# Norm of the latents ahead of the last gate tile's end, a new buffer layout, and head roots spread by rounded hi/lo products

## What is computed

```python
z = h @ w_in
qa, ka, va, cq, ckv, kpe, gate = jnp.split(z, ATT_SPLITS, axis=-1)
cq = _rmsnorm(cq, g_qa)                  # 512 latents
q_nope = jnp.einsum('bsc,chd->bshd', cq, w_uq)
q_pe = _rope(jnp.einsum('bsc,chr->bshr', cq, w_uqr), pos)
ckv = _rmsnorm(ckv, g_kva)
kpe = _rope(kpe[:, :, None, :], pos)[:, :, 0, :]
...
o_a = _diff_attention(qa, k_all, v_all, lam, q_chunk, k_chunk)
o_a = _rmsnorm(o_a, g_subln, SUBLN_EPS) * (1.0 - lam_init)   # per head
o_lat = _mla_attention(q_lat, q_pe, ckv_all, kpe_all, q_chunk, k_chunk)
o_b = jnp.einsum('bshc,chv->bshv', o_lat, w_uv)
o = jnp.concatenate([o_a, o_b], axis=-1) * jax.nn.silu(gate)
y = o @ w_out
```

## Time and profile before

| | us |
|---|---|
| median of 3 runs | 2079.89 |
| lowest and highest | 2076.95, 2081.9 |
| profiled execution, device time | 2074.99 |
| its span | 2073.2 |
| PE busy | 1850.0 (89%) |
| DVE busy | 1255.5 (61%) |
| ACT busy | 411.3 (20%) |
| POOL busy | 197.4 (10%) |

### The profile page before, as it was taken

The page is one execution under the profiler, slowest core; times in us unless marked ns, Lnnn a source line. Parts: engine busy times, 40 slices in busy tenths (PEclk is TensorE's granted clock), DMA queues, the critical chain, the costliest instruction groups (busy, mean ns, idle before and its releaser), DMA issues.

```text
span 2073.2 us, 32711 instructions
## 1 busy us (share of the span) xinstructions
PE 1850.0 (89%) x13182; PEld 1699.9 (82%) x13182; DVE 1255.5 (61%) x1598; ACT 411.3 (20%) x912; POOL 197.4 (10%) x117
## 2 busy tenths in 40 slices
PE   5548999999999978997987899968999999999995
PEld 0108999999999966776876778957999999999995
DVE  4899667667867653554355544376777544584444
ACT  1241000000010012332355443431000000131111
POOL 2770000000600000000000011210000000001110
PEclk8879999999999999998889898989999999999997
DMA  9555555545655422216134244214444333452222
GB/s 388 226 223 192 205 191 212 193 189 193 238 205 209 182 102 62 62 32 178 60 113 138 84 143 173 91 61 158 180 182 187 126 108 120 163 194 86 81 81 86
DMA packets 86104, 316.04 MB, mean 152 GB/s; under 512 B 12184, under 2 KB 20552, under 8 KB 60448
## 3 DMA queue, kind: packets, MB, share of 16 engines
q1 hardware_dynamic: 64208, 237.70, 31.6%
q10 hardware_dynamic: 21200, 76.48, 10.3%
q0 software_dynamic: 640, 1.10, 0.1%
HBM read 282.56 MB, written 32.69 MB: 152 GB/s over the span
## 4 chain that ended last, share of the span: by engine, by line
PE 66%; DVE 14%; DMA 7%; issue 5%; ACT 5%; POOL 2%; SPq 0%; DVEq 0%; ACTq 0%; POOLq 0%
PE banks L718 66%; DVE banks L1604 3%; DMA w_raw<-in_w_pin 3%; POOL ssq L676 2%; DMA w_adr<-in_w_ada_dve 2%; DMA w_more<-in_w_ada_pe 1%; ACT pxd L1387 1%; DMA d_raw<-pool_d_scratch 1%; DVE w_hi L1566 1%; DVE std L1839 1%; DVE h_lo L395 1%; DVE rstd L1546 1%; DVE x L2034 1%; ACT px L1305 0%; DVE pt_lo L1773 0%
## 5 line engine op out<-in xcount | busy, mean ns | idle before, releaser
L718 PE MATMUL banks<-h_hi,w_hi 128*128 128x272 f32 x3968 | 830.2, 295 | 61.0 <-DVE w_lo L1567 29.5
L718 PE MATMUL banks<-h_lo,w_hi 128*128 128x272 f32 x3712 | 776.4, 291 | 0.0
L718 PE MATMUL banks<-h_hi,w_lo 128*128 128x272 f32 x3456 | 716.1, 289 | 0.0
L718 PEld LDWEIGHTS banks<-h_hi,w_hi 128*128 128x128 f32 x3968 | 630.6, 193 | 72.5 <-issue 45.9
L718 PEld LDWEIGHTS banks<-h_lo,w_hi 128*128 128x128 f32 x3712 | 594.1, 192 | 0.0
L718 PEld LDWEIGHTS banks<-h_hi,w_lo 128*128 128x128 f32 x3456 | 545.5, 190 | 0.0
L1604 DVE CUSTOM_DVE_ANT_0 banks<-w_adr,cond_b 128x2048 f32<-128x2048 f32 x160 | 386.2, 2414 | 19.0 <-DMA w_adr<-in_w_ada_dve 15.8
L1566 DVE CAST w_hi<-w_raw 128x2048 fp32r<-128x2048 f32 x101 | 125.6, 1244 | 219.7 <-PE banks L718 168.2
L1567 DVE TENSOR_TENSOR w_lo<-w_raw,w_hi 128x2048 fp32r<-128x2048 f32 x101 | 249.2, 2467 | 3.5
L1251 ACT ACTIVATE stage<-banks 128x544 f32<-128x544 f32 x48 | 30.1, 627 | 514.4 <-PE banks L718 514.4
L1927 DVE TENSOR_TENSOR x<-x,stage 128x544 f32 (+1 forms) x32 | 23.9, 748 | 168.3 <-ACT stage L1469 168.3
(11 more groups left out here) (293 smaller groups left out, 1696.6 us busy)
## 6 DMA issues: line engine op xcount, KB each, us to landing
w_adr<-in_w_ada_dve ACTq DMA_DIRECT2D x46, 1024.0 KB, 5.0
w_adr<-in_w_ada_dve SPq DMA_DIRECT2D x34, 1024.0 KB, 4.9
w_raw<-in_w_z SPq DMA_DIRECT2D x32, 1024.0 KB, 6.2
w_raw<-in_w_pin SPq DMA_DIRECT2D x32, 1024.0 KB, 6.0
w_raw<-in_w_gate SPq DMA_DIRECT2D x16, 1024.0 KB, 6.9
w_raw<-in_w_out SPq DMA_DIRECT2D x32, 512.0 KB, 3.8
w_raw<-in_w_pout SPq DMA_DIRECT2D x16, 1024.0 KB, 4.8
w_more<-in_w_ada_pe SPq DMA_DIRECT2D x10, 1024.0 KB, 7.4
```

The costliest lines, as they stand in the source:

```text
L718: return pe.matmul(out, lhsT, rhs, start=start, stop=stop)
```

## The change

It has four parts. (1) The sums over partitions and the norm of cq and ckT are put ahead of the last gate tile's end: PE makes the sums between gate tiles 14 and 15, into banks 4 to 7, and no longer waits for the rotation of kpe before the MLA items; ACT's square roots stand between its evictions of these two tiles; DVE works out the norm before it waits for the last tile and its store. SP asks for the first MLA weights after the last adaLN product, and waits for tile and stores only ahead of the gates `sg`. (2) The layout of the MLA and differential scopes is new, so that the factors and the first MLA weights lie over nothing that is still read. The clearing of `qps` comes after the norm. (3) `widen` multiplies rounded operands: `sel_rnd` (rounded by ACT), `rs_hi` and `rs_lo`, four matmuls for a head in place of two in float32, in three bank pairs in place of two; all eight steps of latent half tile 15 come before the first of them. (4) On SP, `qds`, `kds` and `vcs` for the first pair are loaded later, `sel_row` earlier, and the last four rows of x only when all heads are scaled.

```diff
@@ sync @@
-            sp.wait_ge(mm_done, G_OUT)
             sp.wait_ge(adr_used, ADA_P0 + ADA_P1)
-            for s in range(2):
-                sp.wait_ge(stored[s], 16 * (ZT + GT) // 2)
...
                 if t == 0:
+                    sp.wait_ge(mm_done, G_OUT)
+                    for s in range(2):
+                        sp.wait_ge(stored[s], 16 * (ZT + GT) // 2)
                     load_sg(0)
...
             load_head(0)
             load_head(1)
-            for z0, dst in ((ZQ, qds), (ZK, kds), (ZV, vds)):
-                sp.dma_start(dst[:], z_out[z0:z0 + HEADS, :, NP:R].rearrange("h p r -> p h r")).then_inc(new_in, 16)
+            sp.dma_start(vds[:], z_out[ZV:ZV + HEADS, :, NP:R].rearrange("h p r -> p h r")).then_inc(vds_in, 16)
             load_cache(0)
-            load_vcache(0)
...
             sp.wait_ge(ms_fin, 1)
             sp.wait_ge(latent_out, 32)
+            for z0, dst in ((ZQ, qds), (ZK, kds)):
+                sp.dma_start(dst[:], z_out[z0:z0 + HEADS, :, NP:R].rearrange("h p r -> p h r")).then_inc(new_in, 16)
+            load_vcache(0)
...
             sp.wait_ge(df_pv, HEADS)
+            sp.dma_start(sel_row[:], selr).then_inc(df_r_in, 16)
...
             for s in range(2):
                 sp.wait_ge(x1_out[s], 16 * KT // 2)
+            sp.wait_ge(df_scaled, HEADS)
@@ tensor @@
-            big_loop(G_GATE, 0, GT // 2)
-            for s in range(2):
-                pe.wait_ge(acc_free[s], turn_of(G_OUT + (G_OUT + s) % 2))
+            big_loop(G_GATE, 0, GT // 2 - 1)
+            big_wait(G_GATE + GT - 2)
+            big_tile((G_GATE + GT - 2) % 2)
             pe.wait_ge(lat_step, 2 * (2 * LT - 1))
             pe.wait_ge(adr_used, ADA_P0 + ADA_P1)
             for a in range(2):
                 for hf in range(2):
-                    m = small(PS[:, 2 * a + hf, 0:HALF], ones[:], lat_sum[:, a, hf * HALF:(hf + 1) * HALF], True, True)
+                    m = small(PS[:, 4 + 2 * a + hf, 0:HALF], ones[:], lat_sum[:, a, hf * HALF:(hf + 1) * HALF], True, True)
                 m.then_inc(mq_sum, 1)
+            big_wait(G_GATE + GT - 1)
+            big_tile((G_GATE + GT - 1) % 2)
+            pe.wait_ge(mq_var, 2)
...
+            for s in range(2):
+                pe.wait_ge(acc_free[s], turn_of(G_OUT + (G_OUT + s) % 2))
             pe.wait_ge(mq_var, 2)
             pe.wait_ge(mq_norm, 1)
-            pe.wait_ge(kp_done, 1)
...
             def widen(h):
-                b = 4 * (h % 2)
-                if h >= 2:
-                    pe.wait_ge(df_scaled, h - 1)
-                for a in range(2):
-                    m = small(PS[:, b + a, 0:HALF], sel_row[:, h, :], rs8[:, a * HALF:(a + 1) * HALF], True, True)
+                b = (0, 4, 6)[h % 3]
+                if h >= 3:
+                    pe.wait_ge(df_scaled, h - 2)
+                elif h == 2:
+                    pe.wait_ge(acc_free[(G_O2 - 1) % 2], turn_of(G_O2 + 1))
+                for x2, rs in enumerate((rs_hi, rs_lo)):
+                    for a in range(2):
+                        m = small(PS[:, b + a, 0:HALF], sel_rnd[:, h, :], rs[:, a * HALF:(a + 1) * HALF], x2 == 0, x2 == 1)
                 m.then_inc(df_wide, 1)
-            pe.wait_ge(df_rs, 1)
-            pe.wait_ge(df_r_in, 16)
-            widen(0)
-            widen(1)
             latent_half(15, range(4, HEADS))
-            widen(2)
-            widen(3)
+            pe.wait_ge(df_rs, 2)
+            for h in range(4):
+                widen(h)
@@ scalar @@
-            store_loop(G_GATE, GT // 2 - 1, GT // 2, ACT.Silu, g2, 16 * ZT // 2)
+            last_gate(0)
             act.wait_ge(mq_in, 32)
             for a in range(2):
                 act.wait_ge(mq_var, a + 1)
                 act.activation(lat_r[a][:], lat_r[a][:], ACT.Sqrt).then_inc(mq_std, 1)
+            last_gate(1)
+            for s in range(2):
+                act.wait_ge(stored[s], 16 * (ZT + GT) // 2)
             act.wait_ge(kp_done, 1)
...
+            act.wait_ge(df_r_in, 16)
+            act.activation(sel_rnd[:], sel_row[:], ACT.Copy).then_inc(df_sel, 1)
             act.wait_ge(df_var, 1)
...
-            upper(0)
-            upper(1)
             store_half(14)
             evict_half(15)
-            for h in range(2, HEADS):
+            for h in range(HEADS):
                 upper(h)
             store_half(15)
@@ vector @@
-            dve.wait_ge(mm_done, G_OUT)
...
             for a in range(2):
                 dve.wait_ge(mq_sum, a + 1)
-                dve.tensor_scalar(rows(lat_r[a][:]), PS[:, 2 * a:2 * a + 2, 0:HALF], 1.0 / LORA, EPS, ALU.mult,
+                dve.tensor_scalar(rows(lat_r[a][:]), PS[:, 4 + 2 * a:6 + 2 * a, 0:HALF], 1.0 / LORA, EPS, ALU.mult,
...
                 ins.then_inc(mq_norm, 1)
+            dve.wait_ge(mq_norm, 2)
+            dve.memset(lam_in[:, 0, 0:1], 0.0).then_inc(qps_free, 1)
+            dve.wait_ge(mm_done, G_OUT)
...
+            dve.wait_ge(stored[0], 16 * (ZT + GT) // 2)
+            dve.wait_ge(stored[1], 16 * (ZT + GT) // 2)
+            dve.wait_ge(kp_swap, 1)
...
-            dve.reciprocal(rs8[:], rs8[:]).then_inc(df_rs, 1)
+            vchain(dve, dve.reciprocal(rs8[:], rs8[:]))
+            dve.tensor_copy(rs_hi[:], rs8[:]).then_inc(df_rs, 1)
+            dve.wait_ge(df_rs, 1)
+            dve.wait_ge(df_sel, 1)
+            dve.tensor_tensor(rs_lo[:], rs8[:], rs_hi[:].bitcast(F32), ALU.subtract).then_inc(df_rs, 1)
```

More of the change, by code:

```diff
@@ L138, in program @@
         ptd_hi = sb("ptd_hi", [P, 2, QT, NP], F32R, over_ptd)
+        vds = sb("vds", [P, HEADS, NS], scope=over_ptd)
         over_ptd.close()
@@ L272, in program @@
         ml_samp.close()
-        mla.close()
         dif = ExitStack()
@@ L282, in program @@
         sb("half_w", [P, 2 * D], scope=dif)
+        qd = sb("qd", [P, 2, NP], scope=dif)
+        kd = sb("kd", [P, 2, NP], scope=dif)
+        vd = sb("vd", [P, 2, NP], scope=dif)
+        kcs = sb("kcs", [P, 2, PAST], scope=dif)
+        qds = sb("qds", [P, HEADS, NS], scope=dif)
+        kds = sb("kds", [P, HEADS, NS], scope=dif)
+        vcs = sb("vcs", [P, 2, QT, P], scope=dif)
         qd_hi = sb("qd_hi", [P, 2, NP], F32R, dif)
@@ L287, in program @@
         pxds = sb("pxds", [P, SKEYS], scope=dif)
-        sb("rest_of_sample", [P, 608], scope=dif)
-        qd = sb("qd", [P, 2, NP], scope=dif)
-        kd = sb("kd", [P, 2, NP], scope=dif)
-        vd = sb("vd", [P, 2, NP], scope=dif)
-        qds = sb("qds", [P, HEADS, NS], scope=dif)
-        kds = sb("kds", [P, HEADS, NS], scope=dif)
-        vds = sb("vds", [P, HEADS, NS], scope=dif)
-        kcs = sb("kcs", [P, 2, PAST], scope=dif)
-        vcs = sb("vcs", [P, 2, QT, P], scope=dif)
         ptds = sb("ptds", [P, KTS, 2, NS], scope=dif)
         ptd1 = sb("ptd1", [P, KTS, 2, NS], scope=dif)
-        sb("under_cond", [P, 1600], scope=dif)
+        sb("under_cond", [P, 2464], scope=dif)
         rs8 = sb("rs8", [HEADS, R], scope=dif)
@@ L950, in _ @@
             pe.wait_ge(ms_fin, 1)
-            pe.wait_ge(new_in, 48)
+            pe.wait_ge(vds_in, 16)
             for h in range(HEADS):
@@ L1258, in _, with last_gate @@
             store_loop(G_GATE, 0, GT // 2 - 1, ACT.Silu, g2, 16 * ZT // 2, ADA_P0 + ZT)
-            store_loop(G_GATE, GT // 2 - 1, GT // 2, ACT.Silu, g2, 16 * ZT // 2)
+            def last_gate(s):
+                g = G_GATE + GT - 2 + s
+                act.wait_ge(mm_done, g + 1)
+                act.activation(rows(stage[:, s]), acc[g % 2], ACT.Silu).then_inc(acc_free[g % 2], 1)
+                act.wait_ge(acc_free[g % 2], turn_of(g + 2))
+                act.dma_start(g_scr[GT - 2 + s], stage[:, s]).then_inc(stored[s], 16)
+            last_gate(0)
             act.wait_ge(mq_in, 32)
@@ L1704, in _ @@
                 ins.then_inc(mq_norm, 1)
+            dve.wait_ge(mq_norm, 2)
+            dve.memset(lam_in[:, 0, 0:1], 0.0).then_inc(qps_free, 1)
+            dve.wait_ge(mm_done, G_OUT)
+            for s in range(2):
+                dve.wait_ge(acc_free[s], turn_of(G_OUT + (G_OUT + s) % 2))
+            dve.wait_ge(stored[0], 16 * (ZT + GT) // 2)
+            dve.wait_ge(stored[1], 16 * (ZT + GT) // 2)
+            dve.wait_ge(kp_swap, 1)
+            dve.tensor_tensor(rows(qpr[:]), PS[:, 6:8, 0:HALF], rows(sin_t[:]), ALU.mult)
+            vchain(dve, dve.tensor_tensor(kpe[:], kpe[:], cos_t[:], ALU.mult))
+            dve.tensor_tensor(kpe[:], kpe[:], qpr[:], ALU.add).then_inc(kp_done, 1)
             dve.wait_ge(qps_zero, 1)
```

42 lines of the change are left out of this document (20 added, 22 removed).

## The result

The changed kernel takes 2070.49 us (median of 6 runs, 2067.18 to 2072.73); the kernel before took 2079.9 us beside it. The ratio is 0.9959, 95% interval [0.9947, 0.9972]: faster, clear of noise, by 8.5 us by the ratio and 9.4 us by the medians, about half of the 18.5 us forecast, and 2.5 us above the top of the range.

A forecast was written before the change was run, and what follows sets the result against it. TensorE holds 66% of the span, so time is won where the chain leaves it: before item 1 and before half tile 2. 11.5 + 7.0 = 18.5 us off the 2079.9 median gives 2061.4 us, range 2057 to 2068.

The forecast's parts named there:

- Change 1: Norm of cq and ckT moved under the last gate tile, so MLA item 1 starts earlier: 11.5 us gained.
- Item 1 starts at 761.7: MLA item 1, after the last gate tile's store and kpe's rotation, starts at 761.7 instead of 773.26.
- At the full-clock length of 3.92 us: MLA item 0, started at about 755.2, takes 3.92 us, ends at 759.1 and doesn't delay item 1.
- rival D: Slower: TensorE enters MLA units or second output pass at 1.2 GHz and stays; 50 us of it gives 2086; chance 0.05.
- Change 2: Spreads of the heads' roots as rounded matmuls, all after latent tile 15: head 7 earlier, 7.0 us gained.
- So 0.55 us a spread at full clock: Each spread, four rounded matmuls, takes 0.55 us at full clock and about 1.0 at half, against 1.05 and 2.18.
- Products of head 0 start at 1252.1, where they start today: After the first spreads, VectorE's scaling, split and subtraction leave head 0's start unchanged, against 1252.14 today.
- So I expect it to come back among the heads, with no row that shows this mixture: TensorE's clock is half for the first heads, then full; head 7 at about 1259.7, 7.0 us gained.
- rival A: Clock stays at half through all heads: change 2 gives only 4.0 us, 15.5 in all, 2064.4; chance 0.2.
- the case of full clock: Full clock through all heads: VectorE sets the pace, 8.1 us from the heads, 19.6 in all, 2060.3; chance 0.15.
- What follows head 7 stays: 11.5 us to half tile 2.: Behind head 7, unchanged: 0.76 us to the store of x, then 11.5 us to half tile 2.
- three signs of being wrong: VectorE's norm past the store's landing; clock 0.50 throughout the heads; weight load behind the x rows over 5.83 us.

The follow-up runs named there:

- table_early: Changed kernel plus one unused single-element root ahead of ScalarE's wait for the latents' mean square, so the root's table loads early: 2069.25 us, ratio 0.9952.
- filler_item: Changed kernel plus 24 unused full-width rounded matmuls in TensorE's idle time between MLA items 0 and 1: 2071.99 us, ratio 0.9955.
- norm_only: Changed kernel with the heads' part undone (plain float32 spreads, old order and banks), early norm, layout and moved loads kept: 2073.16 us, ratio 0.9967.
- again: The changed kernel unaltered, run and profiled a second time: 2072.09 us.
- order_kept: Changed kernel with rounded spreads kept but their old order and two banks put back, first two ahead of latent tile 15: 2066.19 us, ratio 0.9938.
- wide_alone: Changed kernel with the spreads' operands on all 128 partitions, selector zero below the eight rows, factors 1 there: 2066.05 us, ratio 0.994.
- pad_after: Changed kernel plus 24 unused 32-column products after MLA items where TensorE waits, to move the code packet: 2067.75 us, ratio 0.9951.
- wide: Changed kernel with old spread order, half tile 2's weights loaded ahead of the waits, and spread operands on all 128 partitions: 2059.61 us, ratio 0.9908.

## Why the prediction was half right

**Change 1, place and length.** "So tile 15 ends at 754.05" and "Item 1 starts at 761.7": the sums were put at 740.1, 21.6 us ahead of item 1, and it is 22.3 us. The early sums, item 0 under the string and the store as the last thing to end came as said. The table load didn't: it begins only when VectorE's mean square is there (743.48, idle before it <-DVE lat_r), so the norm took 16.8 us from the sums instead of 15.6. The store's landing, 16.8 us after the sums by the trace and 16.7 by the prediction, covered that, as `table_early` shows: norm and store end together, so the cover had nothing left. The 0.7 us are the waits between the steps behind the landing, 5.5 us instead of the 4.9 I summed. 10.8 us of the 11.5 are real.

**Change 1, what comes next.** "At the full-clock length of 3.92 us" was right for item 0 (3.89), and for item 1 I had no term. Before, it was item 0 that ran at the low clock, 5.58 us in the shade of the norm; rival D's argument against a low clock ("though a pause of nine us lay between them") passed over it, for the pause was followed by item 0 and not by item 1. Now the clock falls in item 1. With the old place of the norm, item 1 to item 2 is 5.63 or 5.64 us in three kernels of three; with the new place it is 5.64 in one of eleven executions, 7.09 to 8.68 in ten, 7.53 on average. That is 1.9 us. TensorE is idle for 3.5 to 3.6 us ahead of item 1 with the new place (2.63 in `filler_item`) and for 1.73 to 2.88 with the old; but the one execution that kept its clock, `norm_only`, had 3.6 us of it too, so the pause alone doesn't decide and the cause is open. Full-width filler with 2.63 us of idle time behind it didn't keep the clock up; whether filler up to item 1 would is open.

**Change 2, the price of a spread.** "So 0.55 us a spread at full clock" was right (0.50), and at half clock it is 1.20 us, not 1.0. A head takes 2.86 us, not 2.65.

**Change 2, head 0.** "Products of head 0 start at 1252.1, where they start today": 0.9 us late. The term that failed is the split of half tile 0, "1.22 us": it took 2.33, with GpSimd's add running beside it from 1239.44. In `again` the split came first and took 1.22, and the subtraction of head 0 behind it took 1.85 instead of 0.71; so the add costs head 0 its 1.1 us either way, and the sum had put it at nothing. The step before that, taking the order as given, missed the larger point: the same spreads in the old order have head 0 on its way 2.2 us earlier (`order_kept`).

**Change 2, the clock.** "So I expect it to come back among the heads, with no row that shows this mixture" is the step that failed. It fell at 1241.3 and came back at 1258.3, 4 us behind head 7. This is rival A: 4.0 us, less 0.9 for head 0 and 0.9 for the slower pace, is 2.2; the traces have 40.76 - 38.63 = 2.1. I had reasoned that 8-row work of 0.55 to 1.0 us between two heads' products, instead of 2.1, would let it come back. It didn't at 1.20 us in each 2.86. `wide_alone` shows that these rows are what counts: with full height the clock stays up, through as much waiting. The argument against the case of full clock ("8-row work and waiting in a row") was half right: the 8-row work is needed for the fall, the waiting is not.

**Behind head 7.** "What follows head 7 stays: 11.5 us to half tile 2." It is 12.7 us, and the cause isn't in this stage: a packet of code falls into the weight load. It does so wherever the norm is early, unless filler moves it (table above). The gate tiles written out of their loop make TensorE's program longer; that this is what moves the packet is likely, as 24 further products in the same program moved it again (`pad_after`), and was not tested by itself. The stage behind it costs another 1.0 us on average: 85.4 us with the late start (six executions: 85.86 to 85.99 in four, and 84.28 and 84.47), 84.3 to 84.5 with the early one (five of five). In the four the clock falls for 3.4 us, as 1268 to 1272 shows at 0.57. TensorE had been idle for 2.15 to 3.41 us ahead of half tile 2 in these, and for 0.55 to 1.87 in the other seven. That the gap makes it fall is likely by these counts and was not tested by itself.

The sum, as forecast and as the runs have it (us):

| term | forecast | measured |
|---|---|---|
| item 1 earlier | 11.5 | 10.8 |
| head 7 earlier | 7.0 | 2.1 |
| item 1 at the low clock | 0 | -1.9 |
| weight load behind a code packet | 0 | -1.2 |
| clock at the start of half tile 2 | 0 | -1.0 |
| sum | 18.5 | 8.8 |

The medians give 9.4; the 0.6 us between is less than two executions of one kernel differ by. Of the signs by which I said it would show, the sums between the tiles and the spreads of 0.5 us at full clock came. So did two of the three signs of being wrong: the clock row of 0.50 throughout the heads, and a weight load of over 5.83 us.

## What to carry to other kernels

Where a row of small products stands between full ones and the clock row shows 1.2 GHz without idle time, give the small ones all 128 rows, zeros in the selector: here it cost two clearings and gave 4.0 us by the ratios (`wide_alone` against the changed kernel); only 8 rows against 128 were tried. With the old order and the early weight load the kernel is 19 us faster than the one before (`wide`, 0.9908). When a transfer on the path is longer by a fixed amount after an edit elsewhere, look at the instruction queues in its stretch before looking for contention of data. And when a stall is removed, ask which of the pieces that ran in its shade at the low clock now stands in the open.

## What the runs showed of the hardware

- TensorE's granted clock was low (0.50, 1241 to 1258 in after) while 8-row products stood among full ones, from head 0 on without a pause, and so in twelve executions of twelve. It stayed at 1.00 when the same products had 128 rows, with 1.77 us idle in the 4 us from 1243 (`wide_alone`), in two of two. The Trainium skill ("TensorE: Matmul & The Clock Gate", Part 1) says that the gate goes by how busy the array has been. If busy means time with an instruction running, this case speaks against it: TensorE was busy for 4.00 of 4 us from 1250 to 1254 of after, at 0.50.
- One packet of program code (0.02 MB) that meets a transfer of 512 KB makes its last part land 1.2 us later (7.01 for 5.76 us), and a store of 272 KB 2.1 us later (4.2 for 2.1). The Trainium skill ("Runtime: NRT & Kernel Launch", Instruction fetch mechanics) calls the cost of crossing a block of code mostly hidden. For TensorE the trace of after agrees, as its matmuls follow one another without a gap from 1258.31 to 1264.84, with the packet at 1262.1; the transfer that it meets is what pays.
- A VectorE operation on two SBUF tiles beside a GpSimd add was held up: 2.33 us instead of 1.22, and in `order_kept` 1.63 instead of 0.71. The Trainium skill ("SBUF — State Buffer", Who interferes with whom) says that a VectorE instruction with two SBUF inputs contends with a GpSimd one that reads SBUF, over a pair of ports that they share, and that the later one is blocked until the first is done. The traces agree: in after the add came 0.10 us ahead of the split and the split lost 1.11 us, most of the add's 1.35; in `again` the split came first and kept its 1.22 us, and the add took 2.31.
- ScalarE's table load did not start while ScalarE waited for the operand of the operation behind it (1.17 us idle up to 743.48 in after). With an unused root of one element ahead of the wait it started 0.41 us behind the evict (743.81 in `table_early`), and the first root came 0.72 us after its operand instead of 1.36.
